# Five half parts of the first modulations move from VectorE to TensorE, and the first slab's lower part from GpSimd to VectorE

## What is computed

```python
c_act = silu(c)                                 # [1024]
mod = c_act @ ada_w[0] + ada_b[0]               # ada_w[0]: [1024, 6*1024]
sh_a, sc_a, g_a, sh_f, sc_f, g_f = split(mod, 6)
h = rms_norm(x, norm_g[0, 0]) * (1.0 + sc_a) + sh_a
y = moba_attention(h, moba_w_qkv[0], ...)
```

## Time and profile before

| | |
|---|---|
| median of 3 runs | 999.32 us (998.53 to 1002.67) |
| the profiled execution | 1001.52 us, of which its span is 999.7 us |
| TensorE matmuls busy | 921.0 us, 92% of the span |
| VectorE busy | 684.4 us, 68% |
| ScalarE busy | 489.5 us, 49% |
| GpSimd busy | 64.8 us, 6% |
| first slab matmul starts | 41.09 us after the span's start |

### The profile page before, as it was taken

How to read it: one execution, slowest core, us unless ns; L and a number is a source line. 1 busy time by engine, 2 the same in 40 slices (tenths; PEclk the granted TensorE clock), 3 DMA queues, 4 the chain that set the end, 5 groups by cost and what they waited for, 6 DMA issues and landing times.

```text
span 999.7 us, 14170 instructions
## 1 busy us (share of the span) xinstructions
PE 921.0 (92%) x5984; PEld 840.0 (84%) x5987; DVE 684.4 (68%) x766; ACT 489.5 (49%) x645; POOL 64.8 (6%) x105
## 2 busy tenths in 40 slices
PE   0799999979999999999999999999869899999995
PEld 0798987969999887998789999998768799999974
DVE  5779965958788866887776654556994645555465
ACT  2545545534334356877564434336652544443453
POOL 2301010201001100000000100000320000000000
PEclk9999999989999999999999999999979899999999
DMA  8999781888889953544468855562533455565511
GB/s 338 315 362 336 277 272 43 288 301 313 286 327 348 314 184 128 166 130 144 152 228 297 272 179 196 177 202 89 166 123 127 159 189 200 175 204 206 204 55 42
DMA packets 125761, 212.73 MB, mean 213 GB/s; under 512 B 4753, under 2 KB 93954, under 8 KB 125698
## 3 DMA queue, kind: packets, MB, share of 16 engines
q1 hardware_dynamic: 113362, 164.63, 48.8%
q0 software_dynamic: 12336, 47.20, 13.1%
HBM read 210.75 MB, written 1.06 MB: 212 GB/s over the span
## 4 chain that ended last, share of the span: by engine, by line
PE 74%; DVE 11%; ACT 7%; DMA 5%; issue 2%; SPq 0%; DVEq 0%; ACTq 0%
PE ps L598 23%; PE ps L599 22%; PE ps L600 22%; DVE w_lo L1481 4%; ACT w_hi L1068 3%; DMA raw<-in_moba_w_qkv 2%; DVE ada_sum L1499 2%; DMA raw<-in_ffn_w_in 1%; DMA ada_raw<-in_ada_w 1%; ACT yg L1110 1%; PE ps L851 1%; PE ps L720 1%; DVE ada_sum L1981 1%; ACT h_hi L1104 1%; DVE ada_sum L1496 1%
## 5 line engine op out<-in xcount | busy, mean ns | idle before, releaser
L1481 DVE TENSOR_TENSOR w_lo<-raw,w_hi 128x2048 fp32r<-128x2048 f32 x140 | 320.3, 2289 | 182.4 <-ACT w_hi L1068 182.2
L1068 ACT ACTIVATE w_hi<-raw 128x2048 fp32r<-128x2048 f32 x145 | 276.8, 1911 | 244.8 <-PE ps L600 205.0
L598 PE MATMUL ps<-h_hi,w_hi 128*128 128x256 f32 x1144 | 326.7, 286 | 1.0 <-DVE w_lo L1481 1.0
L599 PE MATMUL ps<-h_lo,w_hi 128*128 128x256 f32 x1144 | 324.9, 284 | 0.0
L600 PE MATMUL ps<-h_hi,w_lo 128*128 128x256 f32 x1144 | 324.8, 284 | 0.0
L598 PEld LDWEIGHTS ps<-h_hi,w_hi 128*128 128x128 f32 x1144 | 220.8, 193 | 3.4 <-DVE w_lo L1481 2.2
L599 PEld LDWEIGHTS ps<-h_lo,w_hi 128*128 128x128 f32 x1144 | 220.6, 193 | 1.2
L600 PEld LDWEIGHTS ps<-h_hi,w_lo 128*128 128x128 f32 x1144 | 220.5, 193 | 0.0
L598 PE MATMUL ps<-w_hi,o_hi 128*128 128x512 f32 x264 | 108.3, 410 | 12.7 <-DVE o_lo L1878 7.2
L599 PE MATMUL ps<-w_lo,o_hi 128*128 128x512 f32 x264 | 105.5, 400 | 0.0
L600 PE MATMUL ps<-w_hi,o_lo 128*128 128x512 f32 x264 | 105.2, 398 | 0.0
(11 more groups left out here) (296 smaller groups left out, 1107.4 us busy)
## 6 DMA issues: line engine op xcount, KB each, us to landing
raw<-in_ffn_w_in SPq DMA_DIRECT2D x40, 1024.0 KB, 5.9
ada_raw<-in_ada_w POOLq DMA_DIRECT2D x28, 1024.0 KB, 8.5
raw<-in_ffn_w_out SPq DMA_DIRECT2D x22, 1024.0 KB, 5.1
raw<-in_w_up SPq DMA_DIRECT2D x16, 1024.0 KB, 5.3
raw<-in_w_down SPq DMA_DIRECT2D x16, 1024.0 KB, 4.8
raw<-in_moba_w_qkv SPq DMA_DIRECT2D x12, 1024.0 KB, 9.3
yg<-in_ada_w POOLq DMA_DIRECT2D x12, 1024.0 KB, 7.6
raw<-in_diff_w_qkv SPq DMA_DIRECT2D x10, 1024.0 KB, 5.0
```

Of the source, the lines that this page charges most:

```text
L598: T.matmul(out_ap, hi_s, hi_m, start=start, stop=False, skip_group_check=True)
L599: T.matmul(out_ap, hi_s, lo_m, start=False, stop=False, skip_group_check=True)
L1068: A.activation(w_hi[:, n.place], raw[:, n.raw_place], ACT.Copy).then_inc(slab_hi, 1)
L1481: V.tensor_tensor(w_lo[:, n.place], raw[:, n.raw_place], w_hi[:, n.place].bitcast(F32), ALU.subtract).then_inc(slab_lo, 1)
```

## The change

Five half parts, both of m = 2, both of m = 5 and the second of m = 7 (`BY_TENSOR`), are no longer multiplied by VectorE. TensorE takes them as they lie (`direct`): the stationary operand is a 128x128 block of the loaded piece itself, the moving operand the column of `c_act`, and eight matmuls for each half part add into the PSUM columns in which `direct_end` then sums `ada_sum`, as `reduce_mods` did. A semaphore `direct_done` counts 1 behind m = 2, 2 behind m = 5, 3 behind m = 7. The order of the two rows is turned: the scale comes first, then the shift. VectorE's order is now `ada` 0, 1, 3, `x_inverse`, `ada` 4, `mod(SC_A)`, `ada` 6, `tabB`, `ada` 7 (its first half part), gain, `mod(SH_A)`. The lower part of slab 0 is made by VectorE between its first part of `h` and the two low parts of `h`. The load of slab 2 waits for `direct_done` 2, the attention bias and the later `ada` loads for `direct_done` 3.

```diff
-ADA = [(0, m // 4, m % 4, (m + 1) % 3, m // 4) for m in range(8)]
+FIRST_TWO = (SC_A, SH_A)
+ADA = [(0, FIRST_TWO[m // 4], m % 4, (m + 1) % 3, m // 4) for m in range(8)]
...
+BY_TENSOR = ((2, 0), (2, 1), (5, 0), (5, 1), (7, 1))
+def summed(m, k=0):
+    return 2 * m + k - sum(block < (m, k) for block in BY_TENSOR)
...
@@ SyncE
-                    sp.wait_ge(ada_acc, 2 * (n.first + 4))
+                    if n.first + 3 == BY_TENSOR[2][0]:
+                        sp.wait_ge(direct_done, 2)
+                    else:
+                        sp.wait_ge(ada_acc, summed(n.first + 4))
...
@@ GpSimd
+                if m == FIRST_MODS:
+                    pool.wait_ge(direct_done, 3)
-                pool.wait_ge(ada_acc, 2 * max(ada_last(m) + 1, min(m - 2, FIRST_MODS)))
+                pool.wait_ge(ada_acc, summed(max(ada_last(m) + 1, min(m - 2, FIRST_MODS))))
...
-            split_lo(Slab(0))
-
-            pool.wait_ge(ada_acc, 2 * FIRST_MODS)
+            pool.wait_ge(direct_done, 3)
+            pool.wait_ge(ada_acc, summed(FIRST_MODS))
             pool.dma_start(bias[:], ...)
...
@@ TensorE
+            def direct(bank, m, ks, first):
+                pe.wait_ge(first_mods[m], 16)
+                for k in ks:
+                    at = 2 * ADA[m][2] + k
+                    for t in range(KT):
+                        last = T.matmul(ps[:, bank, t:t + 1], first_mod_place(m)[:, k, t * P:(t + 1) * P],
+                                        c_act[:, at:at + 1], start=first and k == 0 and t == 0, stop=False,
+                                        skip_group_check=True)
+                last.then_inc(direct_done, 1)
+            def direct_end(bank, slot):
+                for t in range(KT):
+                    last = T.matmul(ps[:, bank, t:t + 1], ada_sum[:, slot, t * P:(t + 1) * P], ones[:, 0:1],
+                                    start=False, stop=t == KT - 1, skip_group_check=True)
+                last.then_inc(ada_reduced, 1)
+            direct(0, 2, range(2), True)
+            pe.wait_ge(ada_acc, summed(4))
+            direct_end(0, 0)
             pe.wait_ge(xs_ready, 4)
             for t, c in BY_HALF:
                 turn_scaled(0, t, c)
             pe.wait_ge(rows_loaded, 16 * N_VECTORS)
             T.transpose(ps[:, 2, 0:P], rowsB, ident[:]).then_inc(tab_turned, 1)
-            pe.wait_ge(ada_acc, 2 * 4)
-            reduce_mods(1, (0,))
-            pe.wait_ge(ada_acc, 2 * 8)
-            reduce_mods(0, (1,))
+            direct(1, 5, range(2), True)
+            direct(1, 7, (1,), False)
+            pe.wait_ge(ada_acc, summed(8))
+            direct_end(1, 1)
...
@@ ScalarE
             act.wait_ge(gain_ready, 1)
+            act.wait_ge(mod_ready, 2)
             t_modulated(0, 1, 1, 0, gain[:, 0], SH_A)
...
@@ VectorE
                 for k in range(2):
+                    if (m, k) in BY_TENSOR:
+                        continue
...
-            for m in range(8):
-                if m == 4: ...
-                    for t in range(ST):
-                        x_inverse(0, t)
-                if m == 7: ...
-                    V.tensor_copy(tabB[:], ps[:, 2, 0:P]).then_inc(tab_ready, 1)
-                ada(m)
-            dve.wait_ge(ada_reduced, 1)
-            mod(SH_A, ps[:, 1, 0:KT])
-            dve.wait_ge(ada_reduced, 2)
-            mod(SC_A, ps[:, 0, 0:KT])
-            gain_of(0, 2)
+            for m in (0, 1, 3):
+                ada(m)
+            for t in range(ST):
+                x_inverse(0, t)
+            ada(4)
+            dve.wait_ge(ada_reduced, 1)
+            mod(SC_A, ps[:, 0, 0:KT])
+            ada(6)
+            dve.wait_ge(tab_turned, 2)
+            V.tensor_copy(tabB[:], ps[:, 2, 0:P]).then_inc(tab_ready, 1)
+            ada(7)
+            gain_of(0, 1)
+            dve.wait_ge(ada_reduced, 2)
+            mod(SH_A, ps[:, 1, 0:KT])
             t_modulated(0, 0, 0, 0, gain[:, 0], SH_A)
+            split_lo(Slab(0))
             lo_part(0, 0, 0, 0)
             lo_part(0, 1, 1, 0)
             ...
-            dve.wait_ge(slab_lo, 1)
             split_lo(Slab(1))
```

More of the change, by code:

```diff
@@ L346, in build @@
         first_done, tok_ready, tok_turned = sem("first_done"), sem("tok_ready"), sem("tok_turned")
+        direct_done = sem("direct_done")
         rstd_spread, rstd_ready = sem("rstd_spread"), sem("rstd_ready")
@@ L434, in first_mod @@
                 if m == 6:
-                    sp.wait_ge(ada_acc, 2)
-                sp.dma_start(first_mod_place(m), rows(ada_w[0][:, ds(m // 4 * D, D)], m % 4)).then_inc(first_mods[m], 16)
+                    sp.wait_ge(ada_acc, summed(1))
+                sp.dma_start(first_mod_place(m), rows(ada_w[0][:, ds(ADA[m][1] * D, D)], ADA[m][2])).then_inc(first_mods[m], 16)
             first_mod(0)
@@ L543, in load_gate_rows @@
                 pool.wait_ge(h_ready, 4 * (b + 1))
-                pool.wait_ge(ada_acc, 2 * (ADA_LATER, ADA_GA, ADA_GA, len(ADA))[b])
+                pool.wait_ge(ada_acc, summed((ADA_LATER, ADA_GA, ADA_GA, len(ADA))[b]))
                 if b:
@@ L780, in _ @@
                 .then_inc(rel_turned, 1)
+            pe.wait_ge(const_ready, 3)
+            pe.wait_ge(rel_ready, 1)
+            pe.wait_ge(tab_ready, 1)
+            pe.wait_ge(c_ready, 1)
+            def direct(bank, m, ks, first):
[15 more added lines that the diff above has]
+            direct_end(0, 0)
             pe.wait_ge(xs_ready, 4)
@@ L785, in _ @@
             T.transpose(ps[:, 2, 0:P], rowsB, ident[:]).then_inc(tab_turned, 1)
-            pe.wait_ge(const_ready, 3)
-            pe.wait_ge(rel_ready, 1)
-            pe.wait_ge(ada_acc, 2 * 4)
-            reduce_mods(1, (0,))
-            pe.wait_ge(tab_ready, 1)
-            pe.wait_ge(ada_acc, 2 * 8)
-            reduce_mods(0, (1,))
+            direct(1, 5, range(2), True)
+            direct(1, 7, (1,), False)
+            pe.wait_ge(ada_acc, summed(8))
+            direct_end(1, 1)
             pe.wait_ge(mod_ready, 2)
@@ L1118, in gate_hi @@
             def gate_hi(b):
-                act.wait_ge(ada_acc, 2 * (GATE_PART[b] + 1))
+                act.wait_ge(ada_acc, summed(GATE_PART[b] + 1))
                 if b == 1:
@@ L1322, in _ @@
                         i = chunk // 2 - 1
-                        act.wait_ge(ada_acc, 2 * (ADA_LATER + 5 * i + 4))
+                        act.wait_ge(ada_acc, summed(ADA_LATER + 5 * i + 4))
                         act.wait_ge(ada_reduced, i + 4)
@@ L1497, in ada @@
                     else:
-                        dve.wait_ge(ada_acc, m * 2 + k)
+                        dve.wait_ge(ada_acc, summed(m, k))
                         V.scalar_tensor_tensor(out=ada_sum[:, slot], in0=buffer[:, k], scalar=scalar,
@@ L1624, in _ @@
             dve.wait_ge(c_ready, 1)
-            for m in range(8):
-                if m == 4:
-                    dve.wait_ge(ident_step, 2)
-                    for t in range(ST):
-                        x_inverse(0, t)
-                if m == 7:
-                    dve.wait_ge(tab_turned, 2)
-                    V.tensor_copy(tabB[:], ps[:, 2, 0:P]).then_inc(tab_ready, 1)
+            for m in (0, 1, 3):
                 ada(m)
+            dve.wait_ge(ident_step, 2)
+            for t in range(ST):
+                x_inverse(0, t)
+            ada(4)
             dve.wait_ge(ada_reduced, 1)
+            mod(SC_A, ps[:, 0, 0:KT])
[3 more added lines that the diff above has]
+            ada(7)
+            dve.wait_ge(tab_ready, 2)
+            gain_of(0, 1)
+            dve.wait_ge(ada_reduced, 2)
             mod(SH_A, ps[:, 1, 0:KT])
-            dve.wait_ge(ada_reduced, 2)
-            mod(SC_A, ps[:, 0, 0:KT])
-            dve.wait_ge(tab_ready, 2)
-            gain_of(0, 2)
             dve.wait_ge(gain_ready, 1)
+            dve.wait_ge(mod_ready, 2)
             t_modulated(0, 0, 0, 0, gain[:, 0], SH_A)
+            split_lo(Slab(0))
             lo_part(0, 0, 0, 0)
```

## The result

The changed kernel takes 1003.61 us (median of 16 runs, 1001.43 to 1006.81) against 999.57 (16 runs, 995.83 to 1002.67): ratio 1.0039, 95% interval 1.0025 to 1.0053, so 2.5 to 5.3 us slower. 1002.6 was forecast, slower by 3.3 and within 0.5%. Timed once more in a later session it gave 1.0032 (1.0016 to 1.0048).

A forecast was written before the change was run, and what follows sets the result against it. It took TensorE's stream of slabs as the bound, with matmuls busy 92% of the span. First slab 5.7 us late less 2.4 regained made 3.3 slower: from the median of 999.32 to 1002.6 us, range 998.5 to 1006.5.

The forecast's parts named there:

- The passes' price: TensorE's 80 added single-column passes in the prologue: 0.213 us each, 17.1 us in all.
- the slow end: Pass rate at the 1.2 GHz level: 17.1 us for 80 passes, against about 8.6 at the fast rate.
- The order on TensorE: Prologue sequence of direct parts and transposes from 15.34 us, ending at 42.9; parts of `h` at 43.2, 4.8 us late.
- The first rival: Direct passes run at the fast rate: first slab at 36.3 us, 4.8 early, total 995.8 us; chance 12%.
- The split in line: Slab 0's lower part on VectorE costs 2.29 us in line; first slab matmul at 46.8 us, 5.7 late.
- What came back: TensorE's 2.43 us gap at 77.78 us, a wait for slab 7: 1.7 to 2.4 us regained, 2.4 taken.
- The sum of 3.3: Whole kernel: 5.7 us late at the first slab less 2.4 regained, so 3.3 us slower.
- The second rival: Nothing is regained at the gap near 78 us: 5.7 us slower, 1005.0 us; chance 22%.
- The third rival: The prologue doesn't matter, since the chain from 48 to 75 us runs over transfers: about 999.3 us; chance 4%.
- GpSimd's transfers: Attention bias and two `ada` loads on the POOL queue start at 39.3 us against 38.3, costing nothing.
- the load of slab 7: Transfer ahead of the gap near 78 us: issued at 64.7 to 67.2, 12.1 us long, landing at 76.8 to 79.3.

The follow-up runs named there:

- Warm first: The changed kernel with 36 unused bfloat16 matmuls of 512 columns ahead of the first `direct`; ratio to the kernel before 1.0000.
- order only: The changed kernel with no direct part on TensorE, all 16 half parts on VectorE; ratio to the kernel before 1.0001.
- the pure delay: The kernel before with 13 more single-column matmuls, sums unused, ahead of the second `reduce_mods`; ratio to the kernel before 1.0012.
- before again: The kernel before, unchanged, timed and profiled a second time; ratio 0.9987.
- order only, again: Second execution of the changed kernel with no direct part on TensorE; ratio to the kernel before 0.9984.
- one half, again: Second execution of the changed kernel with only m = 5's first half part on TensorE; 996.88 us against 999.51, ratio 0.9971.

## Why the prediction was right

- **The passes' price** held: 0.213 us each, where the clock did not rise. The choice of the slow end came from two facts of the trace before, passes behind transposes that stayed slow and a granted clock that fell within them. "Warm first" shows that such passes, once slow, stayed so for 25 us.
- **The order on TensorE** held line by line in the execution without the fast stretch. The first rival, all passes fast, did not come; a part of it did, about 2.8 us in one of two profiled executions. I had given this no share. The 16 runs may show it too: the six with a mean granted clock of 0.972 to 0.974 average 1002.2 us, the ten with 0.979 to 0.984 average 1004.2; in the repetition seven with the lower clock average 1001.8, five with the higher 1004.5. In "order only", where VectorE sets the first slab, the runs with the lower clock are not the faster ones (six at 999.4, six at 998.2). The profiled execution with the stretch had 0.972 and the one without 0.982, but the prologue of the other runs was not looked at.
- **The split in line** cost what was forecast at the first slab, 47.1 and then 0.25 us of issue.
- **What came back** is the gap: 2.4 to 2.7 us in both executions, 2.4 with 0.7 in the pure delay. The sum of 3.3 is inside the measured 2.5 to 5.3. The second rival (nothing comes back, 5.7 us, ratio 1.0057) lies outside the intervals of both sessions, though not far; what settles it is that no trace of the changed kernel has the gap. The third rival (the prologue doesn't matter) would be 1.000 and is outside both intervals too. GpSimd's transfers came as forecast, at 37.4 and 40.4 us for 39.3, since GpSimd waits for m = 7 on TensorE.
- **Mis-sized: the load of slab 7.** With the old 12.1 us it was to land at 76.8 to 79.3. It took 11.2 and 9.3 us and landed at 74.7 and 75.9, ahead of that range, so the gap was gone with over 1 us to spare. Issued at 59.7 to 66.5 us, this load took 9.3 to 13.8 us over all the traces; what sets it stays open.
- **In part luck: how near the number is.** By the marks an execution as forecast loses 3.6 us and one with the stretch 0.8. Weighted six to ten like the runs above that is 2.6, where the medians say 4.0 and, the second time, about 3.2. Their intervals hold all of these.
- The profiled spans, 999.6 and 999.7, are equal, and still the medians differ by 4: the execution traced for the changed kernel, 1001.43 us, is the fastest of its 16, with the stretch, and the one traced for the kernel before, 1001.52, is 2.0 us above its median.

## What to carry to other kernels

Work moved to an engine that "has time" is free only in that engine's idle stretches, so lay the pieces into them one by one: here the half parts of m = 2 cost nothing, one of m = 5 made the first slab 1.6 us earlier, and all five made it 2.5 to 5.5 us later and cost 0.4%. In such a prologue price single-column matmuls at the slow clock: unbroken, they ran 27 us at the slow pitch in one execution here. But keep a share for a fast stretch, and look at more than one execution. And read a lateness at two marks: a wait for a transfer downstream can give back what was lost upstream, and it can be there in one execution and not in the next.

## What the runs showed that was not expected

At 142 us, every kernel has 32 single-column passes between matmuls of 512 columns. In the kernel before the clock fell there, for 6.8 us; in the changed kernel for 3.4; in "before again", the same program as the first, it did not (the first line is from the kernel before):

```profile
145.40:152.10 6.70, 6.70 (x22) 5.74 (x22) 2.60 (x4) 1.39 (x2) 0.00 (x0) 0.50 0.60 168
```

```profile
142.00:146.00 4.00, 4.00 (x36) 3.89 (x34) 0.00 (x0) 2.44 (x2) 0.00 (x0) 1.00 1.10 348
146.00:152.00 6.00, 6.00 (x27) 4.94 (x28) 3.38 (x6) 1.69 (x4) 0.00 (x0) 1.00 0.70 215
```

A stretch of 6.8 us at half the clock costs about 3.4 us, and there are more such places: behind the scores the clock records have 38.6 us at 0.50 in the kernel before and 28.9 in "before again". At half speed the difference is worth 4.9 us, an estimate, and the two executions differ by 3.7 us behind the scores and by 4.2 in all (1001.52 and 997.36 us). So here the clock can be all of it. It is not all of what makes runs differ: "order only, again" and "one half, again", with 35.2 us at 0.50 each, took 920.1 and 917.8 us behind the scores. That is why a difference of 0.3% needed marks in the trace beside the medians.
